# Sigmoid of a gate from exp and ln on ACT in place of reciprocals on DVE, in a two-layer attention trunk

## The reference

```
proj = rms_norm(x, g) @ w_in
q, k, v, z = split(proj)
q, k = rms_norm of each head (layer 0: then rotary)
y = causal softmax attention of each head (layer 1: with a forget bias)
y = merge_heads(y) * silu(z)
x = x + y @ w_out
```

## Time and profile before

| | |
|---|---|
| median of 3 runs | 563.07 us (563.05 to 563.96) |
| the profiled execution | 564.51 us, its span 562.5 us |
| busy, share of the span | PE 97%, DVE 73%, ACT 51%, POOL 52% |
| granted TensorE clock, mean | 0.997 |

### The profile page before, as it was taken

How to read it: one execution, slowest core, us unless ns; L and a number is a source line. 1 busy time by engine, 2 the same in 40 slices (tenths; PEclk the granted TensorE clock), 3 DMA queues, 4 the chain that set the end, 5 groups by cost and what they waited for, 6 DMA issues and landing times.

```text
span 562.5 us, 9740 instructions
## 1 busy us (share of the span) xinstructions
PE 545.7 (97%) x2958; PEld 499.9 (89%) x2958; DVE 408.6 (73%) x1039; ACT 286.6 (51%) x841; POOL 294.1 (52%) x348
## 2 busy tenths in 40 slices
PE   6998999999999999999999989999999999999998
PEld 4997999999999999878888989999999999998887
DVE  3799797979797979774363767787869595959321
ACT  5735555555454546453445463736464647373500
POOL 4854545454544444425545576657475756663700
PEclk9999999999999999999999999999999999999999
DMA  9812323131313131204442334423341535141221
GB/s 280 215 49 87 93 58 95 56 95 56 93 56 93 56 93 56 93 8 130 108 102 76 95 90 80 95 76 79 90 112 56 118 50 131 37 131 37 76 93 57
DMA packets 78237, 49.95 MB, mean 89 GB/s; under 512 B 4089, under 2 KB 71417, under 8 KB 78210
## 3 DMA queue, kind: packets, MB, share of 16 engines
q1 hardware_dynamic: 78208, 49.61, 32.6%
q10 hardware_dynamic: 2, 0.00, 0.0%
HBM read 47.48 MB, written 2.11 MB: 88 GB/s over the span
## 4 chain that ended last, share of the span: by engine, by line
PE 52%; DVE 17%; POOL 12%; issue 12%; ACT 3%; DMA 2%; SPq 1%; POOLq 0%; ACTq 0%; DVEq 0%
PE banks L343 14%; PE banks L345 14%; PE banks L344 14%; DVE banks L853 11%; POOL w_lo L1064 8%; PE banks L458 3%; POOL rstd L1082 3%; DVE pT_lo L894 2%; PE banks L444 2%; PE banks L375 1%; DMA w_raw<-in_b_w_in_dram 1%; POOL msq L1080 1%; DMA first_raw<-in_a_w_in_dram 1%; ACT junk L626 1%; PE banks L433 1%
## 5 line engine op out<-in xcount | busy, mean ns | idle before, releaser
L1064 POOL TENSOR_TENSOR w_lo<-w_raw,w_hi 128x512 fp32r<-128x512 f32 x147 | 188.4, 1300 | 94.8 <-ACT w_hi L590 94.8
L343 PE MATMUL banks<-w_hi,hT_hi 128*128 128x384 f32 x512 | 175.2, 342 | 8.7 <-DVE qkn L842 4.6
L345 PE MATMUL banks<-w_hi,hT_lo 128*128 128x384 f32 x512 | 172.2, 336 | 0.0
L344 PE MATMUL banks<-w_lo,hT_hi 128*128 128x384 f32 x512 | 172.2, 336 | 0.0
L853 DVE STREAM_TRANSPOSE banks<-qkn 32x256 f32<-32x256 f32 x256 | 116.6, 456 | 3.5
L343 PEld LDWEIGHTS banks<-w_hi,hT_hi 128*128 128x128 f32 x512 | 96.8, 189 | 13.1 <-DVE qkn L842 7.3
L590 ACT ACTIVATE w_hi<-w_raw 128x512 fp32r<-128x512 f32 x148 | 87.8, 643 | 21.8 <-DMA w_raw<-in_b_w_in_dram 13.9
L344 PEld LDWEIGHTS banks<-w_lo,hT_hi 128*128 128x128 f32 x512 | 97.0, 189 | 0.7
L345 PEld LDWEIGHTS banks<-w_hi,hT_lo 128*128 128x128 f32 x512 | 96.8, 189 | 0.0
L1080 POOL TENSOR_TENSOR msq<-ssq,eps 128x2 f32<-128x2 f32 x64 | 13.9, 218 | 125.0 <-ACT junk L626 125.0
L919 DVE RECIPROCAL gz<-gz 128x128 f32<-128x128 f32 x64 | 58.1, 928 | 0.0
(11 more groups left out here) (108 smaller groups left out, 877.5 us busy)
## 6 DMA issues: line engine op xcount, KB each, us to landing
w_raw<-in_b_w_in_dram SPq DMA_DIRECT2D x64, 256.0 KB, 4.0
w_raw<-in_a_w_in_dram SPq DMA_DIRECT2D x52, 256.0 KB, 2.9
w_raw<-in_w_out_dram SPq DMA_DIRECT2D x32, 256.0 KB, 2.9
first_raw<-in_a_w_in_dram SPq DMA_DIRECT2D x12, 256.0 KB, 5.6
cos_t<-c_rows SPq DMA_DIRECT2D x8, 256.0 KB, 3.7
out_dram<-xs SPq DMA_DIRECT2D x7, 256.0 KB, 2.0
xs<-in_x_dram SPq DMA_DIRECT2D x3, 512.0 KB, 5.8
xs<-in_x_dram SPq DMA_DIRECT2D x2, 256.0 KB, 2.9
```

The costliest lines, as they stand in the source:

```text
L343: pe.matmul(dst, ah, bh, start=first and m == 0, stop=False)
L344: pe.matmul(dst, ah, bl, start=False, stop=False)
L345: mm = pe.matmul(dst, al, bh, start=False, stop=last and m == n - 1)
L1064: pool.tensor_tensor(w_lo[:, slot, k, :], raw, f32(w_hi[:, slot, k, :]), ALU.subtract).then_inc(wlo_set, by)
```

## The change

e = exp(-z) is now bounded by DVE (a minimum with 3e38, in place), and ACT makes 1/(1 + e) as exp(-ln(1 + e)) with two activations in place. The Copy that added 1 and the four reciprocals go; the multiplication by z stays on DVE, after `invert_sums`. The two activations stand in `begin` of ACT, behind `split_y` and ahead of everything else of the period; the bound in `begin` of DVE, behind `gate_y`.

```diff
-                act.wait_ge(ez_set, g + 1)
-                act.activation(gz[:, 0, :], gz[:, 0, :], ACT.Copy, bias=1.0).then_inc(ez1_set, 1)
+
+            def sigma(layer, h):
+
+                g = HEADS * layer + h
+                act.wait_ge(bound_set, g + 1)
+                act.activation(gz[:, 0, :], gz[:, 0, :], ACT.Ln, bias=1.0).then_inc(sigma_set, 1)
+                act.wait_ge(sigma_set, 2 * g + 1)
+                act.activation(gz[:, 0, :], gz[:, 0, :], ACT.Exp, scale=-1.0).then_inc(sigma_set, 1)
...
                 if not isinstance(h, int) or h > 0:
                     split_y(layer, h - 1)
+                sigma(layer, h)
...
-            def silu_part(layer, h, n):
-
-                g = HEADS * layer + h
-                part = gz[:, 0, n * P:(n + 1) * P]
-                if n == 0:
-                    dve.wait_ge(ez1_set, 5 * g + 1)
-                dve.reciprocal(part, part).then_inc(ez1_set, 1)
-                if n == 3:
-                    dve.wait_ge(ez1_set, 5 * g + 5)
-                    wait(dve, ylo_set, g)
-                    dve.tensor_tensor(gz[:, 1, :], banks[:, Z_BANK, :], gz[:, 0, :], ALU.mult).then_inc(gate_set, 1)
+            def bound_e(layer, h):
+
+                g = HEADS * layer + h
+                dve.wait_ge(ez_set, g + 1)
+                dve.tensor_scalar(gz[:, 0, :], gz[:, 0, :], NO_MIN, None, ALU.min).then_inc(bound_set, 1)
+
+            def silu(layer, h):
+
+                g = HEADS * layer + h
+                dve.wait_ge(sigma_set, 2 * g + 2)
+                wait(dve, ylo_set, g)
+                dve.tensor_tensor(gz[:, 1, :], banks[:, Z_BANK, :], gz[:, 0, :], ALU.mult).then_inc(gate_set, 1)
...
                 if late:
                     gate_y(layer, h - 1)
+                bound_e(layer, h)
                 split_qk(layer, h)
...
             def period(layer, h, s):
                 begin(layer, h)
-                silu_part(layer, h, 0)
-                silu_part(layer, h, 1)
                 split_v(layer, h + 1, 1 - s, 0)
                 norm_qk(layer, h + 1, 0)
-                silu_part(layer, h, 2)
                 maxima(layer, h)
                 split_v(layer, h + 1, 1 - s, 1)
                 norm_qk(layer, h + 1, 1)
                 invert_sums(layer, h)
-                silu_part(layer, h, 3)
+                silu(layer, h)
```

More of the change, by code:

```diff
@@ L161, in build_trunk @@
         ez_set = sem("ez_set")
-        ez1_set = sem("ez1_set")
+        bound_set = sem("bound_set")
+        sigma_set = sem("sigma_set")
         gate_set = sem("gate_set")
@@ L1031, in last @@
                 begin(layer, h)
-                silu_part(layer, h, 0)
                 maxima(layer, h)
-                silu_part(layer, h, 1)
                 invert_sums(layer, h)
-                for n in range(2, 4):
-                    silu_part(layer, h, n)
+                silu(layer, h)
                 split_probs(layer, h)
```

## The result

The changed kernel takes 609.79 us (median of 4, 608.92 to 610.34) against 563.37 us for the kernel before (median of 4). The ratio is 1.0821, with a 95% interval of 1.0802 to 1.084: 46 us slower. Its profiled execution took 608.92 us, with a span of 607.1. That is 44.4 us over the profiled execution of before; 42.8 were forecast between these two.

The account below looks back on a forecast made before the run. PE (97% busy) bounded the kernel; ACT's delayed squares would make the chain the bound. 24.2 (layer 0) + 13.3 (layer 1) + 3.3 (its first head) + 2.0 (last heads) = 42.8 us more, giving 606 us; range 597 to 617, widened to 590 to 624.

Parts of the forecast that it names:

- Sigma's price: ACT, behind `split_y`: two loads and activations per head move the squares by 4.03 us.
- The pair of the earlier trace: ACT in the old trace: a load with its activation takes 1.95 us, the pair 3.90, with no drain.
- The chain: Squares to rstd, rotations and next `split_qk`: heads take 31.52 us in layer 0, 29.3 in layer 1.
- What a freed DVE is worth: DVE: 58.1 us of reciprocals go, but nothing in the chain after tile 1's rotation gets shorter.
- The first head of layer 1: The chain already binds there; it takes between 2.2 and 4.0 us more, taken as 3.3.
- The last heads: Last head of each layer: sigma delays ACT's exps by 1.46 us; 1.0 taken per layer, 2.0 in all.
- PE's clock: Clock falls behind PE's idle gaps, 1.8 us each, expected to be swallowed by PE's 2.2 to 4 us to spare.
- PE's clock adds to it: Rival: clock falls delay tile 3's squares or come twice per head, up to 25 us more, 618 to 631; chance 0.09.
- No reload: Rival: Exp and Ln share a table, squares move 1.47 us, layer 0 pays 0.9 per head, 569 us; chance 0.02.
- PE's waits: PE waits for `qkn` twice per head: near 3.7 and 0.5 us in layer 0, 2 in layer 1.
- The rival on the other side: Faster, 557.5 us, if new ACT time ahead of the squares is under 0.9 us; chance 0.03.

Follow-up runs that it names:

- experiment 2: Changed kernel with four 128x128 reciprocals per head put back on DVE as dead work at their old places: 610.16 us, ratio 1.0819.
- experiment 4: Changed kernel with sigma's Ln and Exp moved right behind the Exp of z, the bound made by POOL: 560.14 us, ratio 0.9933.
- experiment 7: Changed kernel with sigma's Exp replaced by a Copy, so only Ln's load stands ahead of the squares: 588.95 us, ratio 1.0463.
- experiment 1: Changed kernel with sigma's Ln and Exp replaced by two Copies, so the heads' table loads are gone: 569.39 us, ratio 1.0098.
- the early sigma: The kernel of experiment 4, the changed kernel with sigma's Ln and Exp in ACT's idle stretch: 560.14 us, ratio 0.9933.

## Why the prediction was right

Side and size were right (606 forecast, 609.8 measured, in the range), and so was the mechanism; experiments 2, 4 and 7 show it, each against a rival.

- *Sigma's price.* Forecast 4.03 us on the squares; 3.90 measured (T + 5.40 against 1.50). The pair of the earlier trace rows carried over to the loop: load, activation, load, activation with no gap above 0.02 us. The Trainium skill, page "ScalarE: Activation LUTs", section "What ACT_TABLE_LOAD costs", gives 1283 ns for the load, and every one of the 32 here agrees; the drain of about 1380 ns that it adds is in none of them. One load for ln and exp, from the same page's section "Table sets: the hidden batching unit", did not come about: there are two per head.
- *The chain.* Layer 0 was forecast at 31.52 and runs at 31.27 where the clock holds; layer 1 at 29.3 and 29.2. Most of the 0.25 lies in the squares (0.13) and in POOL's step from the squares to rstd (1.73 us to its end for 1.84).
- *What a freed DVE is worth.* Forecast as nothing in the chain; shown by experiment 2, within its 1.6 us.
- *The first head of layer 1*: 3.3 forecast, 3.8 measured. *The last heads*: 2.0 forecast, 1.4 measured.
- *PE's clock* is the term that was mis-sized. I wrote that the falls would happen and be swallowed. They happened, and 3.6 us in layer 0 were not swallowed, since PE's spare time lies as a whole ahead of tile 2, while the chain picks PE's results up again at tile 3, with only 0.8 us to spare (in head 3 ACT waited 2.78 - 0.82 = 1.96 us longer for tile 3 than in head 2, and 1.13 of that reached POOL). It is the rival "PE's clock adds to it" at a seventh of its price. A sum over a head's spare time hid that.
- *The total is closer than its terms.* Between the two profiled executions the sum is 1.6 us short (42.8 for 44.4). Layer 0 was 2.0 short, 3.6 from the clock less 1.7 by which seven heads' chain was forecast too long; the first head of layer 1 was 0.5 short, its other heads 0.6 and the last heads 0.6 too high, and 0.6 ahead of the first T was not in the sum. That these nearly cancel is luck. The other 2.2 us between 606 and 609.8 are scatter: I took off 1.4 us because the profiled execution of before lay that much over its median, and the changed kernel's lies 0.9 under its own.
- *The rival "No reload"*, at 569, is what experiment 1 made (569.4), though by another split: 0.52 per head and not 0.9 in layer 0. The prediction reads the Trainium skill's rule of one load for ln and exp in two ways, as one load left in each pair and, in this rival, as none in the loop; with one load ahead of the squares, experiment 7 measures 589.
- *PE's waits.* I expected 3.7 us at tile 2 and 0.5 at tile 3 in layer 0. It is one wait per head, 2.7 to 4.2 us; the one at tile 3 is too short to be listed. Where the clock had fallen in the head before, PE comes 0.8 us later to tile 2 and waits 2.7; behind head 2, where it had held, it waits 3.54, near the forecast.
- *The rival on the other side* held as a statement of where it turns: faster once sigma runs in the idle stretch before T. It gave 557.5 for that; the early sigma measures 560.1 beside a kernel before at 564.4, a gain of 4.2 us (2.4 at equal clock), with 5.6 forecast. The 2.0 us wait of layer 1 did not come back: PE waits 1.99 us there with the early sigma.

## What to carry to other kernels

Price moved work by what stands behind it in its engine's queue, not by the engine's busy share: ACT was half idle, and the same two loads and two activations cost 46 us ahead of the squares and nothing in a stretch of the same period where ACT waits anyway. Functions of ACT that alternate between activation tables cost a load at each switch here, so list the loads from the built program, and look for a form that needs no switch (tanh for a sigmoid did). Before paying to relieve an engine, read what anyone waits for it: here 4.6 us in layer 0 and 2.0 in layer 1, and the three versions that took the reciprocals off DVE without delaying the squares gained 2.3 to 4.2, part of it by PE's clock.

## What the runs showed of the hardware

Filling PE's idle time with 294 useless matmuls made the kernel 4.6 us faster (609.8 to 605.2), as the granted clock's mean rose from 0.972 to 0.997. A load of ACT's table starts ahead of the semaphore wait of the activation that it belongs to (122.66, with the Ln waiting until 124.41), so a load just ahead of a wait is hidden in it. In experiment 7 the load ahead of the exps starts at 143.49, while DVE is still at the maxima that they wait for (until 144.66).
